# A moved weight split, earlier small products and longer runs of filler matmuls in a mixture-of-experts block

## The reference

```python
mod   = silu(c) @ ada_w + ada_b                    # 6 x 1024 modulation values: shift, scale, gate, twice
h     = rms_norm(x) * (1 + scale1) + shift1
proj  = h @ w_in                                   # 1024 x 5376: queries, keys, values, gates of two mixers
o_att = attention(q, k, v)                         # 8 heads, rotary positions
o_hg  = rms_norm(gated_linear_scan(...)) * silu(hgate)      # 4 heads, both directions
merged = sigmoid(g0) * (o_att @ w_branch_att) + sigmoid(g1) * (o_hg @ w_branch_hg)
x     = x + gate1 * (merged @ w_out)
h2    = rms_norm(x) * (1 + scale2) + shift2
top_w, top_idx = top_k(softmax(h2 @ w_router).T, 32)        # each of 16 experts picks 32 tokens
x     = x + gate2 * scatter_add(expert_mlp(h2[top_idx]) * top_w)    # 16 experts, 1024 -> 2048 -> 1024
```

## Time and profile before

| | |
|---|---|
| median of 3 runs | 1835.39 us (1830.55 to 1835.78) |
| the profiled execution | 1830.55 us, its span 1828.4 us |
| TensorE busy, granted clock over the span | 1473.4 us (81%), 0.887 of full |
| VectorE, ScalarE, GpSimd busy | 582.6, 466.8, 91.9 us |
| moved by DMA | 565.31 MB, mean 309 GB/s |
| experts' weights on the move | from 256.6 us to 1214.7 us |

### The profile page before, as it was taken

One profiled execution on the slowest core, in us unless ns is written; L12 is line 12 of the kernel. 1 busy time (PEld: TensorE's weight loads), 2 busy tenths in 40 slices (PEclk: granted clock), 3 DMA queues, 4 the chain that ended last, 5 costly groups with the idle time before them and its releaser, 6 DMA issues.

```text
span 1828.4 us, 21009 instructions
## 1 busy us (share of the span) xinstructions
PE 1473.4 (81%) x8891; PEld 927.3 (51%) x8891; DVE 582.6 (32%) x747; ACT 466.8 (26%) x660; POOL 91.9 (5%) x79
## 2 busy tenths in 40 slices
PE   3999988876667766777667766769899999989998
PEld 1987565322213222122212221228799978868997
DVE  3488364000000000000000000027655555755553
ACT  3676232000000000000000000025554444664442
POOL 2591000000000000000000000000000000000000
PEclk9999998988877778777787878789999999999999
DMA  9536779999999999999999999995455536425550
GB/s 353 170 117 229 220 298 366 429 427 429 428 428 428 429 428 428 428 429 429 427 430 428 429 428 429 428 387 184 152 193 188 190 141 208 150 103 185 184 184 24
DMA packets 97876, 565.31 MB, mean 309 GB/s; under 512 B 4780, under 2 KB 6072, under 8 KB 73240
## 3 DMA queue, kind: packets, MB, share of 16 engines
q1 hardware_dynamic: 95080, 555.81, 75.3%
q0 software_dynamic: 2112, 7.06, 1.2%
q10 hardware_dynamic: 624, 1.57, 0.2%
HBM read 563.37 MB, written 1.05 MB: 309 GB/s over the span
## 4 chain that ended last, share of the span: by engine, by line
DMA 45%; PE 42%; DVE 6%; ACT 4%; issue 3%; POOL 1%; SPq 0%; DVEq 0%; ACTq 0%; POOLq 0%
DMA ring_b<-in_w_exp_down_dram 22%; DMA ring_b<-in_w_exp_up_dram 21%; PE PS L2038 10%; PE PS L2039 10%; PE PS L2040 10%; PE PS L2369 3%; PE PS L2393 3%; DVE parts L1280 2%; PE PS L2021 1%; DMA ring_a<-in_w_branch_att_dram 1%; DMA arena<-in_ada_w_dram 1%; PE PS L2121 1%; ACT parts L791 1%; DVE rounded L1280 1%; ACT junk L809 1%
## 5 line engine op out<-in xcount | busy, mean ns | idle before, releaser
L1280 DVE TENSOR_TENSOR parts<-ring_a,parts 128x2048 fp32r<-128x2048 f32 (+1 forms) x101 | 235.7, 2337 | 159.0 <-ACT parts L791 158.6
L2369 PE MATMUL PS<-ring_a,arena 128*32 128x512 f32 x1232 | 177.7, 708 | 100.7 <-DMA ring_a<-in_w_exp_up_dram 61.2
L791 ACT ACTIVATE parts<-ring_a 128x2048 fp32r<-128x2048 f32 (+1 forms) x101 | 191.1, 1899 | 174.9 <-PE PS L2040 158.5
L2369 PE MATMUL PS<-ring_b,arena 128*32 128x512 f32 x768 | 134.7, 838 | 100.2 <-DMA ring_b<-in_w_exp_up_dram 61.6
L1689 DVE TENSOR_TENSOR arena<-PS,arena 128x512 f32<-128x512 f32 x16 | 11.1, 692 | 564.5 <-PE PS L2369 564.5
L2369 PEld LDWEIGHTS PS<-ring_a,arena 128*32 128x32 f32 x1232 | 36.4, 120 | 236.8 <-DMA ring_a<-in_w_exp_up_dram 102.5
L1016 ACT ACTIVATE arena<-PS 128x512 f32<-128x512 f32 x16 | 9.6, 597 | 564.0 <-PE PS L2369 564.0
L2038 PE MATMUL PS<-parts,hT 128*128 128x512 f32 (+1 forms) x352 | 130.1, 370 | 12.3 <-DVE parts L1280 4.3
L2393 PE MATMUL PS<-ring_b,arena 128*32 128x512 f32 x720 | 102.2, 701 | 44.6 <-DMA ring_b<-in_w_exp_down_dram 44.6
L2038 PE MATMUL PS<-hT,parts 128*128 128x256 f32 x448 | 127.8, 285 | 9.8 <-POOL hT L674 9.8
L2369 PEld LDWEIGHTS PS<-ring_b,arena 128*32 128x32 f32 x768 | 24.7, 133 | 205.3 <-DMA ring_b<-in_w_exp_up_dram 103.0
(11 more groups left out here) (329 smaller groups left out, 2176.6 us busy)
## 6 DMA issues: line engine op xcount, KB each, us to landing
ring_a<-in_w_exp_gate_dram SPq DMA_DIRECT2D x45, 2048.0 KB, 25.6
ring_b<-in_w_exp_down_dram SPq DMA_DIRECT2D x45, 2048.0 KB, 26.0
ring_a<-in_w_exp_up_dram SPq DMA_DIRECT2D x32, 2048.0 KB, 25.2
ring_b<-in_w_exp_up_dram SPq DMA_DIRECT2D x32, 2048.0 KB, 26.6
ring_a<-in_w_exp_down_dram SPq DMA_DIRECT2D x16, 2048.0 KB, 27.1
ring_b<-in_w_exp_gate_dram SPq DMA_DIRECT2D x16, 2048.0 KB, 23.4
ring_a<-in_w_up_dram SPq DMA_DIRECT2D x16, 2048.0 KB, 7.8
ring_a<-in_w_down_dram SPq DMA_DIRECT2D x16, 2048.0 KB, 7.6
```

The costliest lines, as they stand in the source:

```text
L791: act.activation(part_of(c, 0), raw(c), ACT.Copy).then_inc(chunk_high, 1)
L1280: dve.tensor_tensor(part_of(c, 1), raw(c), part_of(c, 0).bitcast(F32), ALU.subtract)\
L2369: ins = mm(PS[32 * j:32 * j + 32, side, :], xe[:, 2 * q + kk, :], w[:, kk, j * NB:(j + 1) * NB], start=q == 0 and kk == 0, stop=q == 3 and ...
```

## The change

It leaves the arithmetic as it is. `adc6` moves ahead of the turning of queries and keys (`turn_qk`), `adc7` between the second and the third score product, and onto another pair of PSUM banks. The second chunk of `W10` is split by both engines after `ohgT` is copied out, no longer ahead of it; on VectorE it also stands behind `ada_part(4)` and `ada_col(9)`. VectorE no longer splits the chunks of `ya0` and `ya1` between the modulation steps of `ada5` and the two rows, but after them. `adr4` and `adr5` exchange their pairs. Both runs of filler grow from two products to six.

```diff
 JOBS:
-    + [..., ("ada6", 1, 1), ("W7", 2, 3), ("lv8", 2, 2)]
-    + [("qT", 2, 0), ("kT", 1, 1), ("adc6", 1, 1), ("ada7", 1, 2), ("sc00", 2, 0), ("sc01", 2, 1), ("sc10", 2, 2), ("sc11", 2, 3)]
-    + [("og", 2, 0), ..., ("pv00", 1, 2), ("pv01", 1, 3), ("adc7", 1, 0), ("ada8", 1, 0)]
+    + [..., ("ada6", 1, 1), ("W7", 2, 3), ("lv8", 2, 2), ("adc6", 1, 1)]
+    + [("qT", 2, 0), ("kT", 1, 1), ("ada7", 1, 2), ("sc00", 2, 0), ("sc01", 2, 1), ("adc7", 1, 2), ("sc10", 2, 2), ("sc11", 2, 3)]
+    + [("og", 2, 0), ..., ("pv00", 1, 2), ("pv01", 1, 3), ("ada8", 1, 0), ("W9", 2, 1)]
-    + [("ada4", 1, 3), ("adc9", 1, 0), ("W10", 2, 3), ("ada5", 1, 0), ("adr4", 1, 2), ("adr5", 1, 0)]
+    + [("ada4", 1, 3), ("adc9", 1, 0), ("W10", 2, 3), ("ada5", 1, 0), ("adr4", 1, 0), ("adr5", 1, 2)]
 ScalarE:
             half_of_turned(3, "PT11")
-            split_to(CHUNK_OF["W10"] + 1)
+            split_to(CHUNK_OF["W10"])
             (the attention's output and ohgT are copied out)
+            split_to(CHUNK_OF["W10"] + 1)
             branch_gate("W9", 1, 0)
             split_to(CHUNK_OF["ya1"])
 VectorE:
             copy_out("lv8", AT[:, 0, 1].rearrange("p h s -> p (h s)"), 0)
+            ada_col(6)
             copy_out("qT", aqT[:, 0:2, :].rearrange("p i s -> p (i s)"), 0)
             ...
             split_to(CHUNK_OF["W8"] + 1)
-            ada_col(6)
             ada_part(7)
             ...
             maxima(1, "sc01")
+            ada_col(7)
             maxima(2, "sc10")
             ...
             attended("pv01", 0, 1)
-            ada_col(7)
             split_to(CHUNK_OF["W9"] + 1)
             ...
             ada_col(8)
-            split_to(CHUNK_OF["W10"] + 1)
+            split_to(CHUNK_OF["W10"])
             attended("pv10", 1, 0)
             ...
             ada_part(4)
             ada_col(9)
-            split_to(CHUNK_OF["ya0"])
+            split_to(CHUNK_OF["W10"] + 1)
             ada_part(5)
             dve.wait_ge(bias1_in, 32)
             ada_row(4, gate1[:, 0:NB])
-            split_to(CHUNK_OF["ya1"])
             ada_row(5, gate1[:, NB:D])
             split_to(CHUNK_OF["yh0"])
 TensorE:
-            natural("W7", hT, lambda: (level(8), turn_qk()))
-            ada_col(6)
+            natural("W7", hT, lambda: (level(8), ada_col(6), turn_qk()))
             ada_part(7)
             ...
             a_scores(0, 1)
+            ada_col(7)
             a_scores(1, 0)
             ...
             a_values(0, 1)
-            ada_col(7)
             ada_part(8)
 between the tiles of nT1:
-                    spin(2, 5)
+                    spin(6, 5)
 ahead of ib0:
-            spin(2, 3)
+            spin(6, 3)
```

## The result

The changed kernel takes 1843.05 us (median of 6 runs, 1841.01 to 1847.40), the kernel before in the same comparison 1836.22 us (6 runs, 1830.55 to 1841.52): 6.8 us slower by the medians, where I had forecast 3.1 us, in a range that ended at 1842. The ratio on record is 1.0053, with a 95% interval from 1.0038 to 1.0069. It is not the quotient of these two medians, which is 1.0037. The record lists 39 runs of the changed kernel in all (1841.01 to 1851.61, median 1846.61), and their mean over the mean of the six runs before gives 1.0054. So the cost is 6.8 us by six runs each, and 9.7 us by the ratio. The path that I had for the tail of the block held; the largest cost lay earlier, where I had not looked for it.

What follows compares the result with a forecast made beforehand. The prediction took the first block up to the router to set the start of a DMA-bound expert stage of fixed length. −0.2 + 1.54 + 1.72 = +3.1 us on the median 1835.39 gave 1838.5 us, range 1832 to 1842.

Steps and rivals of the forecast that it cites:

- `adc6` ahead of the turning: First block, around `W7`: the turning moves 1.57 us later, 0.91 is saved again, so +0.66 us at `ada7`.
- `adc7` between the scores: At the scores: the third product waits for VectorE's sum, `gated_values` starts +3.0 us; −1.76 at `ada8` leaves +1.25.
- the clock there: At the hole ahead of `ya0`: hole shrinks from 6.5 to about 4.9 us, clock falls as before, `ya0` loses +0.6.
- the fourth rival: At the router: the second filler runs at 1.2 GHz, +4.3 us instead of +1.72, in all +5.7, 1841.1 us; chance 10%.
- +1.25: At `ada8`: running sum of the early `adc6` and `adc7`, +3.0 less 1.76 us for the wait that falls away.
- −0.2: At the end of `ya0`: sum of all terms before the two longer fillers, −0.2 us.
- The late chunk of `W10` and VectorE's order: Ahead of `ya0`: `att` issued 7.25 us later, its data only +1.9; the new order lets `ya0` start −0.8.
- my upper bound: At `ya0`: the clock stays slow for 6.8 us, the longest row, making the sum there +1.1 us.
- Both fillers: Between the tiles of `nT1` and ahead of `ib0`: four more products each, +1.54 and +1.72 us.
- The first rival: Router and first expert: the longer filler holds the clock, in all −1.2 us, 1834.2 us; chance 12%.
- The shift is not hidden: Expert stage: it moves one for one with the first block; the rival, a hidden shift, gave 1835.4 us; chance 8%.
- the chance of 15%: Whole kernel: chance of slower by over 0.3%, from the second filler running at 1.2 GHz and the rest of the unseen.

Runs made afterwards that it cites:

- e10: Kernel before with `adc6` alone moved ahead of the turning of queries and keys, plus four filler products in its wait: 1835.76 us, ratio 0.9998.
- e4: Kernel before with `adc6` alone moved ahead of the turning of queries and keys, no added filler: 1840.07 us, ratio 1.0028.
- e3: Kernel before with `adc7` alone moved between the second and third score product, no added filler: 1839.94 us, ratio 1.0023.
- e6: Kernel before with `adc7` alone moved between the second and third score product, plus five filler products in its wait: 1835.17 us, ratio 0.9999.
- e1: Changed kernel with both runs of filler back at two products: 1841.26 us, ratio 1.0030 to the kernel before.
- e8: Kernel before with VectorE's new order around `ada5`, exchanged pairs, and nine filler products ahead of `ya0`: 1828.71 us, ratio 0.9968.
- e11: Changed kernel with both fillers at old length, plus filler in three waits (four ahead of `adc6`, five behind `adc7`, seven ahead of `ya0`): 1833.09 us, ratio 0.9988.
- e5: Kernel before with VectorE's new order around `ada5`, exchanged pairs and the later split of `W10`'s second chunk: 1834.28 us, ratio 0.9991.
- e2: Kernel before with both runs of filler at six products and nothing else changed: 1838.64 us, ratio 1.0015.
- e12: Kernel before with only the second filler, ahead of `ib0`, at six products: 1838.06 us, ratio 1.0012.
- e7: Kernel before with only VectorE's new order around `ada5` and the exchanged pairs: 1833.38 us, ratio 0.9985.
- e9: Kernel before with VectorE's new order, exchanged pairs, nine filler products ahead of `ya0`, and `adc7` moved behind `ada8`: 1830.82 us, ratio 0.9978.

## Why the prediction was wrong

**`adc6` ahead of the turning: the step failed, in size and in kind.** I had +0.66 at `ada7`. The move itself costs 1.9 (e10): my 0.66, the 0.77 of the pair that `adc6` shares with the keys' turning, which the schedule's table names and I did not read, and 0.4 in small gaps. The clock adds 2.8 (e4), which makes 4.65 at `ada7` in e4's trace. By the medians e4 costs 5.0.

**`adc7` between the scores: the shift was right, the clock was missing.** I had +3.0 at `gated_values`, 2.3 of them `adc7`'s own. In e3 `gated_values` starts 4.5 us later than before. It starts 5.07 behind the third product, where in e6, at full clock, it starts 2.90 behind it; without these 2.17 the shift is 2.4, my term. At `ada8`, where the old wait falls away as I had said (in the kernel after no wait stands there), e3 is 3.9 later and I had 0.6 for it, which e6 confirms at full clock: the clock, 3.3 us. By the medians e3 costs 3.9.

**The step that failed.** In "the clock there" I treated the clock only where TensorE has a hole already, and in the fourth rival at the router. The two waits that the change adds I priced by their own length. They are short (2.08 us ahead of `adc6`; 0.91 us behind the eight one-column records of `adc7`), but they stand next to small products, and behind them the clock was at the lower level for 6.8 and 10.2 us. Two moves that I had priced at +1.25 cost 9.3 us in the trace of the kernel after, and all that I had put at −0.2, the change without the longer fillers, costs 5.2 us in e1. That the forecast had the right sign is owed to the fillers. I had even written "every low stretch follows one with little work", and used it only to ask whether the new filler would help. The rule of the Trainium skill that I weighed there ("TensorE: Matmul & The Clock Gate", section "What's actually happening"), that activity releases the throttle, speaks against the change at the two new waits; e6, e10, e8 and e11 agree with it (0.9999, 0.9998, 0.9968 and 0.9988, with the clock at 1.00 there). Being busy was not always enough, though: from 321.9 to 325.3 us TensorE is busy for 3.40 of 3.40 us with the gather's products, and the clock stays at 0.50 until 332.2.

**The late chunk of `W10` and VectorE's order: right in the path, too large in the gain.** `att` is issued at 223.87; less 0.94 for where the trace starts and 9.3 for what came before, that is 5.9 later, and I had 7.25 − 1.25 = 6.0. ScalarE starts its split at 236.98, by the same count 0.8 later, and I had 1.9 − 1.25 = 0.65. The cover was there. `adr5` runs ahead of the hole, no copy stands between the low part and `ya0`, and the clock fell in the hole as I had written. It fell for 6.8 us, my upper bound, and at `ada10` the kernel after has gained 0.5 from `ada9` on, where I had 1.45. The tail alone is worth 0.8 us by the medians (e5), within its interval of nothing.

**Both fillers: right in size.** +1.5 (e2) and +1.8 (e12) measured for 1.54 and 1.72 taken, and 3.6 together in the kernel after from the turning of tile 0 to the first expert's products, the faster line 2325 and the slower gather included. The first rival, that they hold the clock, is out: in the kernel after the clock is at 0.50 from 311.7 to 315.1 and again from 321.9 to 332.2, right behind the longer filler, over the gather and the first expert. The slow second filler did not come about either (six products, 12 records, in 2.75). The shift is not hidden: from the first expert's first products to the last expert's last slab (line 2393, after 2391) 903.0 us pass before and 903.3 after (311.70 to 1214.71 and 326.50 to 1229.78).

**The sum.** By the medians `adc6` 5.0, `adc7` 3.9, tail −0.8 would make 8.0 us, and e1, which has them all, is 5.2 slower. In ratios that is 0.42% against 0.30%, whose interval ends at 0.42%; so the parts may simply add up, or share a fall of the clock. This stays open. In the traces, the 15.5 us of the kernel after are 9.3 for the two moves, −0.5 for the tail, 1.4 at the `w_out` products, 3.6 for the fillers and 1.6 behind the first expert's products; the 1.4 and the 1.6 turn up without the changed lines too, the 1.4 in e7 and e9 and the 1.6 in e7 (1518.6 us).

**The spread.** I had taken it from three runs, 5.2 us; one kernel's runs lie up to 12.9 us apart (e7). That falls of the clock spread them is my reading, and no run tested it. The traces fit it: up to the level's products near 150 us all 14 kernels run the same code, yet they reach them between 149.15 (e11) and 154.91 us (e7). In e7 the clock is at 0.50 from 20.8 to 38.0 us, in e8, which gets there at 149.16, it is at 0.98 in that stretch:

```profile
20.80:38.00 17.20, 16.30 (x80) 9.83 (x76) 1.87 (x5) 0.00 (x0) 0.00 (x0) 0.50 1.05 387
```

```profile
20.80:38.00 17.20, 12.40 (x96) 6.74 (x88) 4.32 (x12) 2.55 (x6) 0.27 (x1) 0.98 1.05 387
```
And the chance of 15% that I gave to slower by over 0.3% was for a mishap at the router, not for this.

## What to carry to other kernels

A short wait that a reordering puts on TensorE can cost more than its length, where small products stand around it: look up the granted clock behind every wait you add, and price the work that follows at the lower level too. If the wait can't be avoided, put filler into that wait, and only there; filler on a stretch where TensorE is already late cost its length here and gave nothing back. Don't price a change by two traces: the same wait lost the clock in one trace and not in another. Before you move a small job, read which PSUM pair it now shares with which neighbour, since that neighbour waits for its consumer.

## What was unexpected of the hardware

A wait of 2.1 us ahead of eight one-column products and ten turnings was enough for 6.8 us at 1.2 GHz (e4, 160.9 to 167.7); the same place with four filler products in the wait had none (e10). In the kernel after, the clock was also at 0.50 from 321.9 on, while the gather's products ran without a gap (busy 3.40 of 3.40 us). Two waits of nearly one length (3.78 us in e5, 4.18 in e7) came out differently in the one execution that I saw of each, and so did one wait of 2.38 us ahead of the `w_out` products, in five traces of 14. Nine products without a result are worth 4.7 us of 1835 by the medians (e8 against e7).
